# A hybrid decoder block with 32 experts on one core: the first expert gathered from unnormalised parts, its block table built inside its body, the first panel issued by two engines, the last expert's gather moved

## What is computed

```python
# x (1, 256, 1024), mem (1, 256, 1024), all float32, one layer
x = x + token_mix(rmsnorm(x, norm_mix_w), ...)       # HGRN2 + GLA heads, w_in (1024 x 3600), w_out
x = x + cross_attend(rmsnorm(x, norm_xa_w), rmsnorm(mem, norm_mem_w), w_xq, w_xkv, w_xo)
x = x + moe(rmsnorm(x, norm_moe_w), ...)
return rmsnorm(x, norm_final_w)

def moe(h2, ...):                                    # 256 tokens, 32 experts, top 4
    logits = h2 @ w_router + b_router
    gates = softmax(top_k(logits, 4))
    # each expert e on the tokens that chose it:
    gu = xb @ w_gate_up[e] + b_gate_up[e]            # 1024 -> 2048
    gate, up = minimum(gu[:, :1024], 7), clip(gu[:, 1024:], -7, 7)
    act = (up + 1) * gate * sigmoid(1.702 * gate)
    yb = act @ w_down[e] + b_down[e]                 # 1024 -> 1024, scaled by the gate, added to the token's row
```

## Time and profile before

| | us |
|---|---|
| median of 3 runs | 1238.4 (1237.03 to 1238.72) |
| the profiled execution, its own time | 1238.16 |
| its span, first to last instruction | 1236.5 |
| outside the span | 1.7 |
| mean granted TensorE clock, share of full | 0.982 |
| PE busy (matmul) | 1165.0, 94% |
| DVE, ACT busy | 266.1, 180.8 |
| HBM read | 443.45 MB |

### The profile page before, as it was taken

The page is one execution under the profiler, slowest core; times in us unless marked ns, Lnnn a source line. Parts: engine busy times, 40 slices in busy tenths (PEclk is TensorE's granted clock), DMA queues, the critical chain, the costliest instruction groups (busy, mean ns, idle before and its releaser), DMA issues.

```text
span 1236.5 us, 16338 instructions
## 1 busy us (share of the span) xinstructions
PE 1165.0 (94%) x6604; PEld 553.0 (45%) x6605; DVE 266.1 (22%) x615; ACT 180.8 (15%) x297; POOL 20.6 (2%) x60
## 2 busy tenths in 40 slices
PE   8999999999899999999999989999899999989986
PEld 5855864874444444443333333333333433333332
DVE  4335454125321111211111111111121111111112
ACT  4322211034211100101000000000010100001002
POOL 3000010010000000000000000000000000000000
PEclk9999999999999999999999999999999999999998
DMA  8943400676899999999999999999999999999995
GB/s 267 375 140 132 136 11 0 233 286 271 307 430 432 428 429 430 430 429 429 431 430 426 428 431 430 430 432 432 431 433 428 431 429 430 435 427 425 426 426 211
DMA packets 44461, 445.17 MB, mean 360 GB/s; under 512 B 6416, under 2 KB 6880, under 8 KB 25760
## 3 DMA queue, kind: packets, MB, share of 16 engines
q1 hardware_dynamic: 43984, 442.92, 85.9%
q0 software_dynamic: 432, 1.59, 0.5%
HBM read 443.45 MB, written 1.05 MB: 359 GB/s over the span
## 4 chain that ended last, share of the span: by engine, by line
PE 58%; DMA 37%; SPq 2%; DVE 1%; ACT 1%; issue 1%; ACTq 0%; DVEq 0%
DMA ring<-in_w_gate_up 36%; PE bank L853 28%; PE bank L595 11%; PE bank L586 7%; PE bank L863 3%; PE bank L874 3%; PE bank L606 2%; PE bank L942 1%; DMA ring<-in_w_in 1%; SPq L433 1%; ACT region L985 1%; PE bank L734 1%; PE bank L933 1%; PE bank L792 1%; PE bank L773 1%
## 5 line engine op out<-in xcount | busy, mean ns | idle before, releaser
L853 PE MATMUL bank<-ring,region 128*64 128x512 f32 x3072 | 694.5, 606 | 53.2 <-DMA ring<-in_w_gate_up 51.7
L853 PEld LDWEIGHTS bank<-ring,region 128*64 128x64 f32 x3072 | 230.0, 139 | 475.7 <-issue 393.4
L1582 DVE TENSOR_SCALAR region<-bank 128x512 f32<-128x512 f32 x32 | 22.1, 692 | 705.8 <-PE bank L853 705.8
L595 PE MATMUL bank<-ring 128*128 128x512 f32 x336 | 147.0, 594 | 0.4 <-ACT ring L985 0.4
L985 ACT ACTIVATE region<-bank 128x512 f32<-128x512 f32 (+1 forms) x136 | 74.0, 545 | 319.7 <-PE bank L853 208.4
L595 PEld LDWEIGHTS bank<-ring 128*128 128x128 f32 x336 | 63.0, 190 | 75.4 <-issue 74.7
L985 ACT ACTIVATE bank<-region 128x512 f32<-128x512 f32 x32 | 19.3, 602 | 508.4 <-DVE region L1582 508.4
L586 PE MATMUL bank<-ring 128*128 128x256 f32 x384 | 84.1, 380 | 0.0
L586 PEld LDWEIGHTS bank<-ring 128*128 128x128 f32 x384 | 72.6, 190 | 9.9
L863 PE MATMUL bank<-region 64*128 64x512 f32 x264 | 65.6, 615 | 0.7 <-ACT region L985 0.7
L874 PEld LDWEIGHTS bank<-region,r_levels 128*128 128x128 bf16 x1584 | 63.0, 117 | 0.4 <-DVE stat L1656 0.3
(11 more groups left out here) (203 smaller groups left out, 443.7 us busy)
## 6 DMA issues: line engine op xcount, KB each, us to landing
ring<-in_w_gate_up SPq DMA_DIRECT2D x50, 4096.0 KB, 32.6
ring<-in_w_down SPq DMA_DIRECT2D x63, 2048.0 KB, 18.8
ring<-in_w_gate_up SPq DMA_DIRECT2D x26, 2048.0 KB, 16.0
ring<-in_w_in SPq DMA_DIRECT2D x6, 2048.0 KB, 18.4
ring<-in_w_xkv SPq DMA_DIRECT2D x4, 2048.0 KB, 10.6
ring<-in_w_out SPq DMA_DIRECT2D x2, 2048.0 KB, 8.3
ring<-in_w_xq SPq DMA_DIRECT2D x2, 2048.0 KB, 7.7
ring<-in_w_xo SPq DMA_DIRECT2D x2, 2048.0 KB, 15.2
```

The lines of the kernel that those rows point to most:

```text
L595: last = pe.matmul(bk[:, :], lhs[:, k, t * P:(t + 1) * P], w[:, k, :], start=(k == 0), stop=(k == KT - 1))
L853: last = pe.matmul(bk[half * ROWS:(half + 1) * ROWS, :], lhs, w[:, half * 512:(half + 1) * 512], start=start, stop=stop, skip_group_check= ...
L1582: v.tensor_scalar(g_t, bank_g[:, :], LIMIT, None, ALU.min).then_inc(sem["g_clamped"], 1)
```

## The change

First panel: ACT issues its first two parts, SP issues both tiles of x and then the third part. PE takes each part for both tiles before it goes on to the next. Four warm-up matmuls of 13 move behind the first transposes. ACT scales mem before it takes `hf`, and `lb_sigmoid` moves back. Newton is one cubic and one quadratic step.

Gate and up bias: four DMAs fill all 128 partitions, no memset; ACT's and DVE's three cutting steps start between `pT` and `pv` instead of behind `pv3`.

Routing: `norm_moe_w` is multiplied into the router's weights (256 columns) instead of into `eT`. The parts are cut from x times the norm row, without the inverse rms, in five `PIECES` (tile, first column, last column) through one buffer; the inverse rms comes back as a multiplication of the gathered columns by `row_scales`, which two float32 matmuls (`scales`) build from `scaled_sel`. `xo11` is computed in two quarters of 256 columns. `seed` is done by ACT copies. SP loads parts of (1,2) and (1,3) as their space comes free.

First expert (`lead=True`): it starts with one block assumed, on the first half of `xbT`; `table_ready`, the gates' transposes and `blocks_of` are waited for inside it, behind gate and up chunk 1 (`one_time`).

Each pass: the bias rows of the next pass move to the end of the pass; DVE instead of ACT takes `bank_a` and multiplies by `row_scales`; `scales` is added. In the last pass the two halves of `gather` stand behind chunks 1 and 2.

End: one row of `norm_final_w` is loaded by SP and broadcast to all partitions by POOL, into a free ring slot; ACT issues one of the four stores.

```diff
+IN_PARTS = {8: 2, 9: 2}
+PIECES = [(0, 0, D // 2), (0, D // 2, D), (1, 0, D // 2), (1, D // 2, 3 * D // 4), (1, 3 * D // 4, D)]
+CUTS = 3
-WARM_UP = 13
+WARM_UP = 9
+FILL = 4
+KEEP_WARM = 2
-KEEP_WARM = 6
...
             load_x(0)
             sp.dma_start(w_mix, ...)
-            for i, k0 in enumerate(FIRST_ROWS[:-1]):
-                if i == 2:
-                    load_x(1)
-                k = slice(k0, FIRST_ROWS[i + 1])
-                sp.dma_start(panel(0)[:, k, :], ...).then_inc(first_in[i], 16)
+            load_x(1)
+            k = slice(FIRST_ROWS[2], KT)
+            sp.dma_start(panel(0)[:, k, :], ...).then_inc(first_in[2], 16)
...
             load_chunk(1, 1)
+            sp.wait_ge(sem["panel_half"], 1)
+            load_cols(1, 2, 0, SLOT // 2)
             wait_full(sp, "xo11")
-            load_chunk(1, 2)
+            load_cols(1, 2, SLOT // 2, SLOT)
+            sp.wait_ge(sem["xw_ready"], len(PIECES))
+            load_cols(1, 3, 0, 3 * D)
             wait_full(sp, "router1")
-            sp.wait_ge(sem["h2_second"], 1)
-            load_chunk(1, 3)
             sp.wait_ge(sem["seeded"], 2 * NT)
-            sp.wait_ge(sem["part1_ready"], 6)
+            sp.wait_ge(sem["cut_ready"], CUTS * len(PIECES))
             load_chunk(1, 4)
-            wait_taken(sp, "table")
+            sp.wait_ge(sem["table_ready"], 1)
...
-            sp.dma_start(final_row, A["norm_final_w"]...broadcast_to([P, D])).then_inc(sem["final_row_in"], 16)
+            sp.dma_start(final_row[0:1, :], A["norm_final_w"]...).then_inc(sem["final_row_in"], 16)
...
+            pool.wait_ge(sem["final_row_in"], 16)
+            pool.partition_broadcast(final_row, final_row[0:1, :], channels=P).then_inc(sem["final_row_ready"], 1)
...
+            for n in range(FILL):
+                pe.matmul(banks[7][:, 0:P], ident[:, :], ident[:, :], start=(n == 0), stop=(n == FILL - 1))
+            for k0, k1 in zip(FIRST_ROWS, FIRST_ROWS[1:]):
+                pe.wait_ge(first_in[FIRST_ROWS.index(k0)], 16)
+                for t in range(NT):
+                    if (t, k0) == (1, 0):
+                        flip_x(1)
+                    for k in range(k0, k1):
+                        last = pe.matmul(rows_bank[t][:, :], hT[:, k, t * P:(t + 1) * P], w[:, k, :], ...)
...
+            w = arrived("w_xo", PW)
+            for q, job in enumerate(("xo11a", "xo11")):
+                for k in range(KT):
+                    if (q, k) == (1, KT // 2):
+                        for k_late in range(4, 6):
+                            last = flip_tile(late_bank, x_res, 1, k_late)
+                    last = pe.matmul(bk[:, 0:QUARTER], oT[:, k, P:T], w[:, k, c], ...)
...
+            pe.matmul(count_psum, chosen[:, 1, :], ...).then_inc(sem["rank_psum"], 1)
+            keep_warm()
+            pe.wait_ge(sem["sel_ready"], 1)
+            pe.wait_ge(sem["cut_ready"], 3 * CUTS)
+            gather(range(KT // 2))
+            pe.wait_ge(sem["scaled_ready"], 1)
+            scales().then_inc(sem["rs_psum"], 1)
+            pe.wait_ge(sem["cut_ready"], len(PIECES) * CUTS)
+            gather(range(KT // 2, KT)).then_inc(sem["xb_psum"], 1)
+            pe.wait_ge(sem["nb_ready"], 1)
+            ... # three table matmuls -> table_psum
+            pe.wait_ge(sem["rs_ready"], 1)
+            bias_of(bank_g, 0)
...
                             last = pair(bank_u, xbT[:, f, :], ...)
                         last.then_inc(sem["chunk_used"], 1)
+                        if final and k in (1, 2):
+                            next_rows(k - 1)
+                        if lead and k == 1:
+                            pe.wait_ge(sem["table_ready"], 1)
+                            pe.reg_load(blocks, table[0:1, 0:1])
+                            pe.wait_ge(sem["gates_ready"], 1)
+                            pe.wait_ge(sem["yb_ready"], w1)
+                            one_time()
...
-                    gather(range(KT // 2, KT)).then_inc(sem["xb_psum"], 1)
+                    if not final:
+                        next_rows(1)
+                    pe.wait_ge(sem["scaled_ready"], pe.snap(w1 + 1))
+                    scales().then_inc(sem["xb_psum"], 1)
...
+                    pe.wait_ge(sem["xb_ready"], pe.snap(w1 + 1))
+                    bias_of(bank_g, 0)
+                    bias_of(bank_u, D)
...
+            for i in range(2):            # ACT
+                act.dma_start(panel(0)[:, k, :], first_panel[:, k, :]).then_inc(first_in[i], 16)
...
-            remember(0)
             for t in range(NT):
                 act.wait_ge(sem["mem_rms"], t + 1)
                 fn(mem_raw[:, t, :], ..., scale=rstd[:, 2 + t:3 + t]).then_inc(sem["mem_scaled"], 1)
+            nc.scalar.preload_act_table_set("sigmoid_and_others")
+            remember(0)
             remember(1)
...
+            choose(1)                     # DVE
+            rest(4, 0)
+            dve.wait_ge(sem["rank_psum"], 1)
+            link(v.scalar_tensor_tensor(rank_m, ranks, 1.0, chosen, ALU.add, ALU.mult))
             select(e0, rows0)
+            rest(4, 1)
+            select_scaled(e0, rows0)
+            ... # nb_col -> nb_ready
+            v.tensor_copy(row_scales, bank_g[:, 0:ROWS]).then_inc(sem["rs_ready"], 1)
+            dve.wait_ge(sem["xb_psum"], 1)
+            scale_xb(0, KT // 2, sem["xb_ready"])
+            gate_weights(1).then_inc(sem["gates_ready"], 1)
+            ... # table -> table_ready
+            scale_xb(KT // 2, KT, sem["xb_rest"])
...
+                dve.wait_ge(sem["xb_psum"], dve.snap(w1 + 1))     # in each pass
+                v.tensor_copy(row_scales, bank_g[:, 0:ROWS]).then_inc(sem["rs_ready"], 1)
+                scale_xb(0, KT, sem["xb_ready"])
```

More of the change, by code:

```diff
@@ L301, in build @@
         out_tile = tm(part(1, 0, SLOT), 0)
+        final_slot = [n for n in range(2, RING) if n not in [slot_of(E - 1, k) for k in range(CHUNKS)]][0]
+        final_row = part(final_slot, 0, D)
         def bank_of(job):
@@ L836, in _ @@
[L836 to L847 removed]
+            w, bk = arrived("w_xo", 0), begin("xo01")
@@ new lines, in _ @@
+            for k in range(KT):
+                if k == KT // 2:
+                    flip_rows("eT", 0, 1, "xo")
+                last = pe.matmul(bk[:, :], oT[:, k, P:T], w[:, k, :], start=(k == 0), stop=(k == KT - 1))
+            end(last, "xo01")
+            pe.wait_ge(sem["router_scaled"], 1)
+            bk = begin("router0")
+            for k in range(KT):
+                await_rows({0: ["eT00"], 4: ["eT01"]}, k)
+                last = pe.matmul(bk[:, 0:E], h2T[:, k, :], w_router[:, k, :], start=(k == 0), stop=(k == KT - 1))
@@ new lines, in route @@
+            def route(k):
+                return pe.matmul(routed[:, 0:E], h2T[:, k, :], w_router[:, k, :], start=(k == 0), stop=(k == KT - 1))
+            routed = begin("router1")
+            wait_taken(pe, "eT10")
+            for k in range(KT // 2):
+                route(k)
+            wait_taken(pe, "xo11")
+            pe.wait_ge(sem["h2T_part"], 1)
+            for k in range(6, KT):
+                last = flip_tile(late_bank, x_res, 1, k)
+            end(last, "eT11")
+            for k in range(KT // 2, KT - 2):
+                route(k)
@@ L849, in pair @@
+            wait_taken(pe, "eT11")
+            for k in range(KT - 2, KT):
+                last = route(k)
+            end(last, "router1")
             def pair(bk, lhs, w, start, stop):
@@ new lines, in _, with one_time, expert, next_rows @@
+            bias_of(bank_g, 0)
+            def one_time():
+                for t in range(NT):
+                    last = pe.transpose(bank_d[:, t * P:(t + 1) * P], selg[:, t, :], ident[:, :])
+                last.then_inc(sem["gT_psum"], 1)
+                pe.wait_ge(sem["spans_ready"], 1)
+                pe.matmul(e_psum, e_col, spans, start=True, stop=True)
+                pe.matmul(first_of_psum, first_col, spans, start=True, stop=True).then_inc(sem["blocks_psum"], 1)
+            def expert(e, slots, counts, last_tile=None, lead=False, final=False):
+                def next_rows(half):
+                    pe.wait_ge(sem["sel_ready"], pe.snap(w1 + 1))
+                    gather(range(half * KT // 2, (half + 1) * KT // 2))
+                if lead:
+                    blocks = pe.alloc_register("blocks_of_lead")
+                    pe.reg_mov(blocks, 1)
+                else:
+                    blocks = pe.value_load(table[0:1, bass.ds(e, 1)], min_val=1, max_val=MAXB)
+                    first = pe.value_load(table[0:1, bass.ds(e + E, 1)], min_val=0, max_val=MAXW)
@@ L1164, in _ @@
-            take("gT", combT, bank_of("gT")[:, 0:T])
-            wait_taken(act, "table")
+            for i in range(CUTS):
+                cut(1, i)
+            half_squared(1, 0)
+            cut(2, 0)
+            cut(2, 1)
+            gate_exps(0)
+            cut(2, 2)
+            seed(0, 0, "xo01")
+            seed(0, 1, "eT01")
+            wait_taken(act, "router0")
```

(2 more changed lines are left out.)

551 lines of the change are left out of this document (293 added, 258 removed), and 2 rows, old and new, of the table JOBS.

## The result

The change made the kernel slower, not faster: 1240.76 us (median of 17 runs, 1236.38 to 1243.41) against 1237.42 for the kernel before (17 runs, 1236.15 to 1238.87). The ratio is 1.0025, with a 95% interval of 1.0017 to 1.0033. The forecast was 1226.8, with 1223.3 to 1231.0 as its range. The profiled execution took 1240.56, its span is 1238.5.

What follows compares the result with a forecast made beforehand. The end was taken as set by when the weight stream becomes continuous, what is left to load, and the tail. Front 2.2, stream 9.0 and tail 0.4 sum to 11.6: 1238.4 - 11.6 = 1226.8 us, range 1223.3 to 1231.0.

Steps and rivals of the forecast that it cites:

- the one on the broadcast: At the end: POOL's broadcast of the final row has 5.7 us before it is needed, so it is hidden.
- Rival C: At the end: the broadcast ends behind 1226.3, each us beyond 5.7 costs a us; at 7.7, 1228.8; chance 0.07.
- The front, 2.2: First panel up to hq0: taking both tiles with each part gains 1.7 to 2.7 us, taken as 2.2.
- Fewer warm-up matmuls cost nothing: At PE's start: fewer warm-up matmuls cost nothing while the first transposes wait for x.
- Routing: From routing to the first expert: first weights at 317.6 in before's time, a gain of 7.5 us on 325.1.
- rival B: First expert starts late or at half clock: stream gains 7.0, sum 9.6, 1228.8 us; chance 0.18.
- A: Before the first expert: a late last cut delays (1,4) and (1,5); stream gains 6, sum 8.6, 1229.8 us; chance 0.12.
- the savings listed as 1.1: In routing, up to `chosen`: narrower addition, square and cut, shorter Newton and later `ngmax` save 1.1 us in all.
- The stream, 9.0: Weight loads around the first expert: continuous stream effectively starts at 323.2 instead of 332.65; gains 9.0 us.
- Passes: Each expert's pass: PE grows to some 26 us, below the stream's 29.3, so the effect is nothing.
- tail: Behind the last weight chunks: the moved gather nets 0.2 us, Newton saves 0.2 to 0.3; 0.4 taken in all.
- rival D: In each pass: a pass over 29.3 us makes PE the bound, each 0.1 more costing 3 us; chance 0.03.

Runs made afterwards that it cites:

- experiment 4: Changed kernel plus a POOL memset and an affine select of 8 columns behind the final broadcast: 1240.48 us, ratio 1.0024.
- experiment 5: Changed kernel with the final row spread by DMA and an 8-column POOL broadcast right behind the first affine select, none at the end: 1229.16 us.
- experiment 6: Changed kernel, broadcast kept, plus one POOL iota of 8 columns behind the final broadcast: 1229.71 us, ratio 0.994.
- experiment 1: Changed kernel with the final norm row spread to all partitions by a DMA, no POOL broadcast: 1227.92 us, ratio 0.993.
- experiment 10: Repeat of the changed kernel with the final row spread by DMA, no POOL broadcast: 1229.77 us, ratio 0.9928.
- experiment 9: Changed kernel with the final row spread by DMA and the last expert's gather moved back to where all others have it: 1229.73 us.
- experiment 7: Changed kernel with the final row spread by DMA and the old front: panel by SP, hf0 whole before hf1, 13 warm-up matmuls: 1229.96 us.
- experiment 3: Kernel before, with only the final row changed: loaded to one partition and broadcast by POOL: 1246.48 us, ratio 1.0072.
- experiment 8: Changed kernel with the final row spread by DMA and all first-panel parts issued by SP in the old order: 1230.62 us.
- experiment 11: Repeat of the changed kernel with the final row spread by DMA and the first panel issued by SP: 1228.97 us.

## Why the prediction was wrong

**The step that failed** is the one on the broadcast: "I take it as hidden", with its bounds "from below it costs nothing, from above the longest POOL operation near it". Both bounds are prices of a place, the end, and there the statement held: 1.30 us, ready 9 us early. But the operation changed POOL's state at the end of an execution, and the next execution paid for it at its start (by the account that fits experiments 4 to 6), ahead of an instruction that the diff does not touch. Rival C had a late broadcast, and looked for it at the end too. The question that was missing is what else this engine has to run with that code, before and after, the next execution included. The price: 11.7 us from the changed kernel to experiments 1 and 10, or 11.1 to experiment 6.

The Trainium skill (GPSIMD Engine Reference, Instruction dispatch) puts the load of code for a fresh POOL kernel at about 6 us. The 6.90 and 7.00 measured in experiments 6 and 5 agree roughly; the 10 to 11.6 at the start are well above it. The prediction applied the rule to the broadcast's own call only, and so came to 0.3 to 2 us.

**The front, 2.2.** Right in kind, a little large. With the hole away, `hq0` starts at 26.66, 26.98, 26.91 and 27.92 (experiments 1, 6, 9 and 10) against 28.96 in the timeline of before (28.79 with the old front of experiment 7): 1.0 to 2.3 earlier, 1.8 in the mean. By the medians it is 0.9. It varies with the first transposes. Behind 13 warm-up matmuls they take 1.04 in all three profiles (before, experiments 3 and 7); behind the 9 of the new order 1.04 to 1.91. "Fewer warm-up matmuls cost nothing" was not right in each execution. In the changed kernel itself the front is moot: PE started at 12.97, and up to `hq0` it no longer waits for a DMA.

**Routing.** Right. Less the front's 2.2 I had (1,4) issued at 313.1 and (1,5) at 318.9. Experiment 1 had 311.28 and, by the end of its row of two issues, 317.0; with the 1.7 of the dip that it did not have, 313.0 and 318.7. The first weight matmul stood at 313.3, 315.0 with the dip, against 315.4. The start of the lead expert (0.6 taken where 1.96 stood), the full clock and the absence of a DMA hole all held: rival B, and A with it, can be set aside. Two small slips in the sums changed nothing: the savings listed as 1.1 add up to 1.0, and rival B's 319.2 should be 319.0 (317.0 and 1.96).

**The stream, 9.0.** Right in kind, too large by some 1.5. Counted from the start of `hq0`, with 1.7 off for each dip, PE takes up chunk (31,2) 6.9 to 8.2 us earlier in the profiles of the eight runs without the hole (experiments 1 and 5 to 11), 7.6 in the mean. Of this 5.1 lie ahead of the issue of (1,4), as forecast (5.0); the rest is 1.8 to 3.2 where the forecast had 4.0. About 1 us of the difference can be read: I had the stream at 430 GB/s from the first byte of (1,5), but it ran below. In experiment 1, around and behind the expert's first chunks:

```profile
315.00:319.00 4.00, 4.00 (x22) 1.36 (x20) 1.15 (x5) 0.00 (x0) 0.00 (x0) 1.00 1.04 406
319.00:323.00 4.00, 4.00 (x24) 1.31 (x22) 1.21 (x5) 0.46 (x2) 0.00 (x0) 1.00 0.98 410
...
331.00:341.00 10.00, 10.00 (x84) 4.88 (x83) 2.15 (x8) 1.21 (x3) 0.00 (x0) 1.00 0.99 411
341.00:391.00 50.00, 50.00 (x324) 20.46 (x322) 10.50 (x26) 3.78 (x7) 0.00 (x0) 1.00 1.01 427
```

From 319 to 391 these rates and those between miss 430 by some 1.0 us in all. What makes up the rest is open. The prediction also took 1.2 us from the issue of (1,5) to its data, which none of its rows shows. In the kernel before, DMA was idle from that issue, at 330.9, to 331.5, and by the prediction's own counting the stream began in effect 1.75 behind it (332.65).

**Passes and tail.** A pass grew by 0.47 instead of 0.2 to 0.3, and cost nothing, as PE still waits for a chunk of weights every 29.2 us. The tail gained 0.2 of the 0.4; the moved gather gave 0.0 of its 0.2 (experiment 9).

**The sum without the hole.** 1.8 + 7.6 + 0.2 = 9.6 by the profiles, and 1237.6 less 1229.0 = 8.6 by the medians, where I had 11.6. So even without the broadcast the forecast would have been about 2 us too low, and the time inside its range. With it, the hole (11 to 12) outweighs all. The chance of 0.03 for the slower side rested on rival D alone, a pass over 29.3; nothing of the kind happened, and the side came true through a state that no rival held.

## What to carry to other kernels

When a change brings a new kind of operation to an engine that runs loaded code, look at the engine's first operation in the next execution too, and not only at the place of the new one: a hole with the releaser "issue" ahead of an untouched line is the sign. If it can't be avoided, end the program with an operation that needs the code its start needs, in time that nobody waits for; or let a DMA spread the row. Here the two do equally well within the noise (1229.7 and 1229.0, against 1240.8). And of gains below 2 us, ask more of medians than of one pair of profiles, whose clock dips are as large.

## What the runs showed of the hardware

- A partition broadcast of 128 x 1024 float32 takes 1.30 to 1.53 us on POOL. An affine select of 128 x 128 takes 0.28.
- Behind a broadcast the next iota waits for what by all signs is a load of code. Where the broadcast is POOL's last operation, the first affine select of an execution waits too. The load took 6.90 and 7.00 us ahead of an iota, with DMA traffic of 53 and 25 GB/s (experiments 6 and 5). At the start of an execution it took 9.99 and 10.47 with SP alone issuing the panel (305 and 298 GB/s), 11.41 and 11.64 with SP and ACT issuing (329 and 334 GB/s). The load ahead of the early broadcast of experiment 5 took 10.04, at 354 GB/s.
- What is loaded stays from one execution to the next, as far as experiments 4 to 6 can tell: with the same broadcast in both programs, the first select starts at 12.63 where nothing follows the broadcast, and at 1.49 where an iota does.
- An affine select that follows the broadcast runs without a load (experiments 4 and 5), so it isn't bound to the code that the iota needs.
- The granted clock between 170 and 180 us was 1.00, 0.83 or 0.66 in executions of nearly the same code, in which PE was busy throughout the stretch. In the kernels with the hole the dip comes some 12 us later, with the work. What decides it was not found.
